# Second attention: blocks of a head from the last to the first, and the causal mask subtracted by VectorE

## The reference

```python
fcum = jnp.cumsum(log_f, axis=-1)
for blk in range(seqlen // ATT_BLOCK):                 # blocks of 128 queries
    q0, q1 = blk * ATT_BLOCK, (blk + 1) * ATT_BLOCK
    s = einsum(q[:, :, q0:q1], k[:, :, :q1]) * scale
    s = s + fcum[:, :, q0:q1, None] - fcum[:, :, None, :q1]
    s = jnp.where(kpos[None, :] <= qpos[:, None], s, -jnp.inf)
    prob = jax.nn.softmax(s, axis=-1)
    outs.append(einsum(prob, v[:, :, :q1]))
```

## Time and profile before

| | |
|---|---|
| time, median of 3 runs | 2604.86 us (2602.79 to 2605.42) |
| the profiled execution's own time | 2604.71 us |
| its span | 2602.9 us |
| granted clock of TensorE, mean | 0.991 |
| TensorE busy (matmul) | 2530.3 us, 97% of the span |
| TensorE weight loads busy | 2120.4 us, 81% |
| VectorE busy | 1580.3 us, 61% |
| ScalarE busy | 1225.1 us, 47% |
| GpSimd busy | 1134.3 us, 44% |

### The profile page before, as it was taken

The page is one execution under the profiler, slowest core; times in us unless marked ns, Lnnn a source line. Parts: engine busy times, 40 slices in busy tenths (PEclk is TensorE's granted clock), DMA queues, the critical chain, the costliest instruction groups (busy, mean ns, idle before and its releaser), DMA issues.

```text
span 2602.9 us, 32821 instructions
## 1 busy us (share of the span) xinstructions
PE 2530.3 (97%) x12946; PEld 2120.4 (81%) x12946; DVE 1580.3 (61%) x2413; ACT 1225.1 (47%) x1858; POOL 1134.3 (44%) x759
## 2 busy tenths in 40 slices
PE   5999999999999999999999999999999999999998
PEld 3788898877888888878788888888888888888886
DVE  7554899487555556665833367665666666654333
ACT  4243888344444443342543435543666666642132
POOL 0222444439787863444487234333322222235233
PEclk8999999999999999999999999999999999999998
DMA  6133001322222226553232322222111111167452
GB/s 272 65 121 130 1 1 66 114 79 92 89 81 78 92 102 242 179 174 122 90 117 102 122 73 90 90 84 71 65 49 49 49 59 60 54 213 273 148 184 97
DMA packets 84457, 275.81 MB, mean 106 GB/s; under 512 B 9392, under 2 KB 9520, under 8 KB 84304
## 3 DMA queue, kind: packets, MB, share of 16 engines
q1 hardware_dynamic: 84304, 273.71, 30.0%
HBM read 219.54 MB, written 54.13 MB: 105 GB/s over the span
## 4 chain that ended last, share of the span: by engine, by line
PE 81%; DVE 9%; ACT 5%; DMA 2%; issue 1%; POOL 1%; SPq 0%; DVEq 0%; ACTq 0%; POOLq 0%
PE ps L614 12%; PE ps L616 12%; PE ps L615 12%; PE ps L991 7%; PE ps L992 7%; PE ps L993 7%; PE ps L857 5%; PE ps L834 4%; PE ps L810 2%; PE ps L811 2%; PE ps L1048 2%; DVE wf L3056 2%; PE ps L1049 2%; PE ps L1050 2%; DVE wf L3081 1%
## 5 line engine op out<-in xcount | busy, mean ns | idle before, releaser
L3383 POOL TENSOR_TENSOR hl<-raw,hl 128x1024 fp32r<-128x1024 f32 x161 | 403.9, 2511 | 933.9 <-ACT hl L1407 933.5
L614 PE MATMUL ps<-ht,hl 128*128 128x512 f32 x1552 | 633.4, 408 | 15.0 <-DVE ht L2456 9.9
L616 PE MATMUL ps<-ht,hl 128*128 128x512 f32 x1552 | 608.3, 392 | 0.0
L615 PE MATMUL ps<-ht,hl 128*128 128x512 f32 x1552 | 607.8, 392 | 0.0
L614 PEld LDWEIGHTS ps<-ht,hl 128*128 128x128 f32 x1552 | 293.5, 189 | 75.4 <-DVE ht L2456 9.9
L616 PEld LDWEIGHTS ps<-ht,hl 128*128 128x128 f32 x1552 | 292.8, 189 | 64.1
L615 PEld LDWEIGHTS ps<-ht,hl 128*128 128x128 f32 x1552 | 294.0, 189 | 53.8 <-issue 1.5
L3459 POOL TENSOR_SCALAR wf<-wf,st 128x1024 f32<-128x1024 f32 (+2 forms) x192 | 168.8, 879 | 318.7 <-DVE st L2589 318.7
L1407 ACT ACTIVATE hl<-raw 128x1024 fp32r<-128x1024 f32 x163 | 171.3, 1053 | 178.9 <-PE ps L1050 66.6
L2396 DVE TENSOR_TENSOR ps<-ps,wf 128x512 f32<-128x512 f32 x116 | 80.8, 697 | 152.3 <-PE ps L993 152.1
L834 PE MATMUL ps<-cst,wf 128*128 128x128 f32 x1088 | 151.4, 274 | 3.8 <-POOL wf L3459 3.8
(11 more groups left out here) (287 smaller groups left out, 5314.8 us busy)
## 6 DMA issues: line engine op xcount, KB each, us to landing
raw<-in_wst SPq DMA_DIRECT2D x243, 512.0 KB, 3.6
wf<-scratch_rows SPq DMA_DIRECT2D x32, 512.0 KB, 5.0
scratch_g<-wf SPq DMA_DIRECT2D x22, 512.0 KB, 2.6
wf<-scratch_g SPq DMA_DIRECT2D x44, 256.0 KB, 4.2
wf<-in_xT SPq DMA_DIRECT2D x16, 512.0 KB, 7.7
htf<-in_wst SPq DMA_DIRECT2D x16, 512.0 KB, 15.4
scratch_ys<-wr SPq DMA_DIRECT2D x16, 512.0 KB, 4.5
ht<-scratch_ys SPq DMA_DIRECT2D x32, 256.0 KB, 5.9
```

The lines of the kernel that those rows point to most:

```text
L614: self.op.matmul(out, wh, xh[:, c], start=(j == 0), stop=False)
L615: self.op.matmul(out, wh, xl[:, c], start=False, stop=False)
L616: t = self.op.matmul(out, wl, xh[:, c], start=False, stop=(j == kt - 1))
L3383: self.op.tensor_tensor(K.hl[:, u * 2048 + 1024:u * 2048 + 2048], K.raw[:, i % 3 * 1024:(i % 3 + 1) * 1024], hi.bitcast(F32), ALU.subtract ...
```

## The change

Three things change, in the second attention only.

1. The matmul with `maskr` on line 815 is gone. VectorE instead subtracts `maskr` from the 128 diagonal columns of the head's running sums, in place, in a new function `mask(h, qt)`, which waits for the sums and for `maskr`; `top` now waits for the label `masked` of its block. Subtracting -1e30 there makes the sums large, and `top` subtracts the sums from the scores.
2. The blocks of a head go from 7 to 0. A block's piece of the tile, once masked, would spoil later blocks that read it unmasked; from the last to the first, each block reads only the pieces up to its own. The pairs for `back` are now (7, 6), (5, 4), (3, 2), (1, 0). VectorE masks block 7 of the pass's first head in step -2, before its first `top`, and after each `top` it masks the next block.
3. `fills` gives other numbers of filler steps to the steps of a pass. Passes 0 to 6 had 0, 2, 3, 3 in steps -2 to 1, and 1, 1, 2, 1, 2, 1, 1, 1, 2, 1, 2, 1 in steps 2 to 13. They now have 1, 2, 3, 3 and 1, 0, 1, 1, 2, 3, 3, 2, 1, 0, 0, 1. The last pass had 0, 3, 3, 3 and 2, 1, 2, 1, 2, 2, 2, 1, 2, 1, 2 (steps 2 to 12), and now has 1, 3, 3, 2 and 1, 1, 1, 1, 3, 3, 3, 2, 1, 1, 1.

```diff
--- before.py
+++ after.py
@@ -529,12 +529,12 @@
 
 
     if s < 2:
-        return (0, 3 if p == 7 else 2, 3, 3)[s + 2]
+        return (1, 3 if p == 7 else 2, 3, 3 if p < 7 else 2)[s + 2]
     if p == 7 and s > LAST_FILL:
         return {13: 1, 14: 4, 16: 3}.get(s, 0) if own else 0
     if p == 7:
-        return (2, 1, 2, 1, 2, 2, 2, 1, 2, 1, 2)[s - 2]
-    return 2 if s in (4, 6, 10, 12) else int(s < 14)
+        return (1, 1, 1, 1, 3, 3, 3, 2, 1, 1, 1)[s - 2]
+    return (1, 0, 1, 1, 2, 3, 3, 2, 1, 0, 0, 1)[s - 2] if s < 14 else 0
 
 
 def steps(n):
@@ -803,17 +803,11 @@
         for half in range((nk + 511) // 512):
             c = slice(half * 512, min(nk, half * 512 + 512))
             out = K.ps[pair][:, c]
-            diag = causal and c.stop == nk
             self.bank_free(2 * pair + half)
             for label in ready:
                 self.wait_ge(*K.at(*label))
             self.op.matmul(out, qs, K.wrr(kh)[:, c], start=True, stop=False)
-            t = self.op.matmul(out, qs, K.wrr(kl)[:, c], start=False, stop=not diag)
-            if diag:
-                self.consts()
-                self.wait_ge(*K.at("maskr"))
-                t = self.op.matmul(K.ps[pair][:, nk - 128:nk], K.idr[:, :], K.maskr[:, :],
-                                   start=False, stop=True)
+            t = self.op.matmul(out, qs, K.wrr(kl)[:, c], start=False, stop=True)
         t.then_inc(*self.done("scores", A, g))
         free = (("top", A, g),) if causal else (("exp", A, g),)
         for half in range((nk + 511) // 512):
@@ -839,9 +833,9 @@
     def back(self, A, g, qt, hi, lo, v, causal, ready, js=None, ahead=None):
 
         K = self.K
-        nk = qt + 1 if causal else 8
+        nk = (qt | 1) + 1 if causal else 8
         for gg in (g - 1, g):
-            for half in range((((qt if gg == g else qt - 1) + 1 if causal else 8) + 3) // 4):
+            for half in range(((qt + g - gg + 1 if causal else 8) + 3) // 4):
                 self.wait_ge(*K.at("plo", A, gg, half))
         for label in ready:
             self.wait_ge(*K.at(*label))
@@ -850,7 +844,7 @@
         if js[0] == 0:
             self.bank_free(b)
         for j in js:
-            c0 = 128 if causal and j == qt else 0
+            c0 = 128 if causal and j == nk - 1 else 0
             for n, m in enumerate((hi, lo)):
                 if ahead and (j, n) == (js[-1], 1):
                     self.wait_ge(*K.at(*ahead))
@@ -1284,7 +1278,7 @@
             def sc(s):
                 h = s // 8
                 k = 2 + 2 * h
-                self.scores(2, 16 * p + s, 2 * p + h, s % 8, h, k, k + 1, True,
+                self.scores(2, 16 * p + s, 2 * p + h, 7 - s % 8, h, k, k + 1, True,
                             (("stacklo", "q2", p, h), ("stacklo", "k", p, h),
                              ("stackhi2", "k", p, h)))
 
@@ -1296,11 +1290,11 @@
                     for _ in range(5):
                         next(late, None)
                 if 0 <= s < 16:
-                    self.turn(2, 16 * p + s, s % 8, 9 + (16 * p + s) % 3, True)
+                    self.turn(2, 16 * p + s, 7 - s % 8, 9 + (16 * p + s) % 3, True)
                 if s >= 2 and s % 2 == 0:
                     g = 16 * p + s - 1
                     hi, lo, _ = pt2(K, (g // 2) % 2)
-                    self.back(2, g, (s - 1) % 8, hi, lo, 6 + (s - 1) // 8, True,
+                    self.back(2, g, 7 - (s - 1) % 8, hi, lo, 6 + (s - 1) // 8, True,
                               (("vstack2", p),))
                 if p == 7 and s == LAST_FILL:
                     self.flush()
@@ -2211,13 +2205,13 @@
                 if g in (0, 2):
                     self.wait_ge(*K.at("stored_ys", 6 + g // 2))
                 if 0 <= s < 16:
-                    self.turn(2, g, s % 8, pt2(K, (g // 2) % 2)[0], True)
+                    self.turn(2, g, 7 - s % 8, pt2(K, (g // 2) % 2)[0], True)
                 if s + 2 < 16:
-                    self.soft(2, g + 2, (s + 2) % 8, 9 + (g + 2) % 3, True)
+                    self.soft(2, g + 2, 7 - (s + 2) % 8, 9 + (g + 2) % 3, True)
                 if s >= 2 and s % 2 == 0:
                     if s == 2 and p:
                         self.wait_ge(*K.at("stored_ya", p - 1))
-                    self.back(2, g - 1, (s - 1) // 8, (s - 1) % 8, w(22))
+                    self.back(2, g - 1, (s - 1) // 8, 7 - (s - 1) % 8, w(22))
                 if s == 15 and p < 7:
                     self.wait_ge(*K.at("scores", 2, g))
                     self.wait_ge(*K.at("qraw", p + 1, 1))
@@ -2573,14 +2567,23 @@
         if causal:
             pw = K.w(p)[:, 0:nk]
             if g >= 3:
-                self.wait_ge(*K.at("turn", A, g - 3, ((g - 3) % 8) // 4))
-            self.wait_ge(*K.at("fcum", h))
+                self.wait_ge(*K.at("turn", A, g - 3, (7 - (g - 3) % 8) // 4))
+            self.wait_ge(*K.at("masked", h, qt))
             self.op.tensor_tensor_reduce(pw, ps, K.w(20 + h % 2)[:, 0:nk], 1.0, -3.0e38,
                                          ALU.subtract, ALU.max, m).then_inc(*self.done("top", A, g))
             self.wait_ge(*K.at("top", A, g))
             self.op.tensor_scalar(m, m, -1.0, None, ALU.mult).then_inc(*self.done("minus", A, g))
         else:
             self.op.tensor_reduce(m, ps, AX, ALU.max, negate=True).then_inc(*self.done("top", A, g))
+
+    def mask(self, h, qt):
+
+        K = self.K
+        c = K.w(20 + h % 2)[:, qt * 128:qt * 128 + 128]
+        self.wait_ge(*K.at("fcum", h))
+        self.wait_ge(*K.at("maskr"))
+        self.op.tensor_tensor(c, c, K.maskr[:, :].bitcast(F32),
+                              ALU.subtract).then_inc(*self.done("masked", h, qt))
 
     def soft(self, A, g):
         K = self.K
@@ -3259,16 +3262,20 @@
                 g = 16 * p + s
                 self.fill(fills(p, s))
                 if s + 2 < 16:
-                    self.top(2, g + 2, 2 * p + (s + 2) // 8, (s + 2) % 8, 9 + (g + 2) % 3, True)
+                    if s == -2:
+                        self.mask(2 * p, 7)
+                    self.top(2, g + 2, 2 * p + (s + 2) // 8, 7 - (s + 2) % 8, 9 + (g + 2) % 3, True)
+                    if s + 3 < 16:
+                        self.mask(2 * p + (s + 3) // 8, 7 - (s + 3) % 8)
                 if late is not None and s + 2 >= 16:
                     for _ in range(5):
                         next(late, None)
                 if 0 <= s < 16:
-                    self.turn(2, g, s % 8, pt2(K, (g // 2) % 2), True)
+                    self.turn(2, g, 7 - s % 8, pt2(K, (g // 2) % 2), True)
                 if s + 2 < 16:
                     self.soft(2, g + 2)
                 if s >= 2 and s % 2 == 0:
-                    self.back(2, g - 1, (s - 1) // 8, (s - 1) % 8, w(22))
+                    self.back(2, g - 1, (s - 1) // 8, 7 - (s - 1) % 8, w(22))
                 if s == 15 and p < 7:
                     self.stack_low(w(23), (0, 1), (0, 1), ("q2", p + 1), 0.125)
                 if p == 7 and s == LAST_FILL:
@@ -3672,7 +3679,7 @@
                     for _ in range(5):
                         next(late, None)
                 if s + 2 < 16:
-                    self.weigh(2, g + 2, (s + 2) % 8, 9 + (g + 2) % 3, True)
+                    self.weigh(2, g + 2, 7 - (s + 2) % 8, 9 + (g + 2) % 3, True)
                 if p == 7 and s == LAST_FILL:
                     self.flush()
```

## The result

| | before | after |
|---|---|---|
| median of the runs, us | 2605.14 | 2628.02 (2626.35 to 2631.15) |
| ratio, 95% interval | | 1.0094 [1.0083, 1.0106] |
| profiled execution, own time, us | 2604.71 | 2626.35 |
| its span, us | 2602.9 | 2624.5 |
| from one store of `ya` to the next, us | 62.84 | 65.93 |

The change makes the kernel slower by 0.94%. The ratio and its interval are estimated from all runs of the two kernels, and so are not exactly the quotient of the two medians. The forecast was slower by 7.4 us, to 2612.1, in a range from 2600 to 2620. The spans of the profiled executions differ by 21.6 us, and 2628.02 lies outside the range.

A forecast was written before the change was run, and what follows sets the result against it. TensorE's instruction stream was taken as the bound: -14.1 us for masks, -2.4 for old waits gone, +22.5 for new waits in passes 0 to 6, +1.4 in the last pass, giving +7.4, 2612.1 us; range 2600 to 2620.

The forecast's parts named there:

- What bounds it: Second attention: TensorE's instruction stream is the time, busy 59.79 of 60 us; a wait put in is lost whole.
- Part 1: Line 815: removing 128 mask matmuls gives back 0.11 us each, -14.1 us in all.
- The rival of 0.06: Line 815: each mask matmul was worth its start distance alone, 0.06 us, so -7.7 us instead of -14.1.
- Part 2: VectorE's 128 new mask subtractions hold it 0.20 us each, 26 us, costing TensorE only where a low part is late.
- The mask is hidden there by 1.4 us or more: Pass start: the first mask fits between VectorE's last product copy and its first `top`, with 1.4 us or more spare.
- Part 3: Reversed block order and new filler places: still 32 filler steps a pass, no cost if nobody waits.
- Part 4: Bank 4 between turns, 2.06 us apart: waits in steps 12, 4, 2 and 10, together 3.2 us in passes 0 to 6.
- Step 2: Passes 0 to 6: the turn in this step waits 0.57 us for its half of bank 4.
- T(1) late behind ScalarE's weight tile: Step 1: ScalarE's 1.06 us weight-tile copy delays the turn's high part, starting 0.95 after the turn instead of 0.64.
- Only the bare distance: Rival: bank 4 waits count without queueing on the engines, 16.8 us against 16.5 gained, 2605 us; chance 0.24.
- No waits: Rival: the turns don't wait, -16.5 us, 2588 us; decides at 2.06 us of waits a pass; chance 0.16.
- Slower by more: Rival: mask matmuls worth only 0.06 us each, -7.7, and a mask operation of 0.28; 2619 us; chance 0.12.

The follow-up runs named there:

- old_order_no_mask: The kernel before without the mask matmul of line 815, mask left out altogether; 2595.85 us, ratio 0.9969.
- best1: The changed kernel with each pass's first mask moved ahead of VectorE's value stack and filler numbers chosen anew; 2599.67 us, ratio 0.9988.
- best1_pe_mask: best1 with the mask by TensorE's old matmul and no mask operation on VectorE; 2605.96 us, ratio 1.0010.
- no_dve_mask: The changed kernel with the mask left out altogether, neither matmul nor VectorE's subtraction; 2618.67 us, ratio 1.0061.
- order_alone: The kernel before with only the blocks' order reversed, mask matmul and old filler numbers kept; 2604.10 us, ratio 1.0003.
- halves_apart: The changed kernel with two filler steps moved so the 16th and 24th end a step (passes 0 to 6); 2618.12 us, ratio 1.0053.
- old_fills: The changed kernel with the filler numbers of the kernel before; 2607.32 us, ratio 1.0014.
- best1_split: best1 with the last store of `ya` issued between the fourth and fifth pair of loads; 2598.90 us, ratio 0.9979.
- best2: best1_split with a filler moved from step 13 to 10 in passes 0 to 6, and other last-pass numbers; 2593.69 us, ratio 0.9957.
- filler_in_12: The changed kernel with one filler step moved from step 8 to step 12 in passes 0 to 6; 2623.72 us, ratio 1.0080.

## Why the prediction was right on the side and wrong in the size

- **What bounds it.** Right. The waits put in were lost whole, as far as the table of starts can tell, which is to some 0.3 us of the 5.2 in a pass.
- **Part 1, -14.1.** Right as a price: 0.12 in old_order_no_mask where I had 0.11. The rival of 0.06 is out. The Trainium skill (TensorE: Matmul & The Clock Gate, Back-to-back issue gap) has 81 ns a matmul of 128 columns; the trace is nearer to 0.11. But a price isn't a gain: old_order_no_mask and best1 (against best1_pe_mask) each kept half of it a pass.
- **Part 2.** The hold of 0.20 was right (0.20 from mask to low part at 2008.71, and 0.2 at steps 4 and 12 in no_dve_mask). The duration was 0.282; the Trainium skill's formula (VectorE: DVE Perf Modes, the section on SBUF-source ops) gives 0.29, so it agrees. "The mask is hidden there by 1.4 us or more" failed: I had put the first mask between the stacks and `top`, which have the time, and did not look at GpSimd, which held it to 1.69. That cost 0.38 a pass at the scores and 0.20 at the copy in step 1. The trace of before already had operations on two SBUF operands that lasted more than three times as long beside GpSimd (L2868, in the section on hardware).
- **Part 3 is the step that failed.** "The fillers are still 32 steps a pass", it says, and "Reordering costs nothing if nobody waits." The order does cost nothing (order_alone). But I counted fillers as interchangeable steps of 0.7 us. They are halves of eight in one bank, and where a half ends inside a step TensorE waits for ScalarE: 1.90 a pass, some 13 us in seven, where the whole miss is 14.2. I had even worked out that 17 steps are done by the end of step 1, and read off it only that a weight tile is copied there. halves_apart shows it: the waits went when one filler step was moved across each of the two ends.
- **Part 4.** Right to 0.1 us in steps 12, 4 and 10. Step 2 was over-estimated by 0.38. The reason that I gave, T(1) late behind ScalarE's weight tile, is of a kind with what happened, but TensorE had stopped in step 1 already, and so ScalarE caught up before T(1). The part's list was of bank 4 alone.
- **Rivals.** "Only the bare distance" is out: steps 4 and 12 took 0.94 and 1.59, not 0.57 and 1.33. "No waits" is out: 5.2 us of waits a pass against the 2.06 from which it decides. "Slower by more" came out on its side and for another reason than it gave.
- **Last pass and after.** Forecast 1.4 of waits against 1.76 of masks, so shorter; measured 1.6 longer and 1.4 more behind it. In the last pass of after TensorE waits six times, 1.4 us for bank 4, 0.6 for L3227 (another hand-over of a half that the fillers make themselves) and 0.2 for the first `top`; with 0.15 for each place that is 3.1, less 1.76 for the masks. The store is issued 0.25 behind VectorE's last copy, since the loads are ahead of it. Together that gives the 1.6. The 1.4 behind it goes with the new wait of 1.8 for the reloaded `ya`: its store lands after 8.0 us, not 5.2. The prediction had no term for either.

The sum again, by the two profiled executions. Passes 1 to 6 were forecast at +1.1 and measured at +3.09 each: 11.9 more than forecast. The first pass grew by 2.2 (from its first scores, 1835.12 in after and 1837.26 in before, to its store): 1.1 more. The last pass and what follows it grew by 3.0 where 0.4 less was forecast: 3.4 more. That the second attention began 2.1 us earlier in after, in work that the change doesn't touch, takes 2.1 off. Together 14.3, and the miss is 14.2. Without that chance difference ahead of it the forecast would have been off by 2 us more.

## What to carry to other kernels

Before filler work is redistributed around a bound engine, write down for each buffer that this work itself hands over where in the sequence the hand-over falls, and keep other work of the engine between it and the next use; here two filler steps on the wrong side of it cost 10 us a kernel. Where an engine waits for a buffer's release, compute the distance through the engines that release it, with what queues on each: it gave three of the four waits here to a tenth of a microsecond, and work moved into one of them was free. And when instructions are taken off an engine that runs close to such distances, the distances have to be re-opened in the same change, or part of the gain turns into waits, here half of it in two pairs of kernels.

## What the runs showed of the hardware

**A VectorE operation on two SBUF operands that starts during a GpSimd operation lasts until that one ends.** In after the first mask of a pass took 1.18 us in the first pass and 1.68 to 1.70 in the seven others, instead of 0.28; the one shown above ended 0.15 behind GpSimd's L3390. Short GpSimd operations do it in small: a mask at 1986.15 took 0.38, beside a weighing of 0.59 that began at 1985.81. Of the 128 masks of after 71 began during a GpSimd operation, and every one of them ended 0.12 to 0.26 behind it; no mask that began outside one took more than 0.30. The same stands in the trace of before, in a subtraction of 512 columns with both operands in SBUF (the view of its line):
```profile
L2868 DVE TENSOR_TENSOR wr<-wf,wr x44: 678/2474/2886, 973.0 to 1198.8; 128x512 fp32r<-128x512 f32 x44
```
It takes 0.68 or 0.69 by itself, and 2.3 to 2.9 where it begins during GpSimd's L3383, ending some 0.55 behind it. Which of the two starts first decides. In best1, a usual pass, VectorE first:
```profile
2036.07 0.28 DVE L2585 TENSOR_TENSOR wf<-wf,maskr 128x128 f32<-128x128 f32 x1
...
2036.17 2.45 POOL L3389 TENSOR_TENSOR hl<-raw,hl 128x1024 fp32r<-128x1024 f32 x1
```
and the one pass that was 0.87 longer, GpSimd first:
```profile
2097.71 2.40 POOL L3389 TENSOR_TENSOR hl<-raw,hl 128x1024 fp32r<-128x1024 f32 x1
...
2097.98 2.27 DVE L2585 TENSOR_TENSOR wf<-wf,maskr 128x128 f32<-128x128 f32 x1
```
Against GpSimd's start VectorE's differs by 0.37 us, and the price by 2 us, with the next turn late. old_fills has a mask of 2.29 at 2100.34 in the same way and that pass is 1.4 longer; halves_apart, best1_split and best2 have one such pass each as well (2.44, 2.27 and 2.29 us; 1.3, 0.9 and 0.9 longer). The Trainium skill (GPSIMD Engine Reference, Specifications) says that GpSimd and VectorE share their SBUF interface and contend when VectorE reads two SBUF inputs; the trace agrees, and shows the size here. A low part, with one operand in PSUM, isn't held: the two at 1979.39 in after took 1.16 together, as in the earlier trace rows, all inside a GpSimd operation of 2.39 from 1978.30. So the move of the mask from TensorE, where the 128 matmuls of before lasted 0.22 to 0.28 us each, to VectorE brought a cost that depends on a race of tenths of a microsecond.

**A store right behind sixteen loads lands late.** SyncE's queue took 9.1 to 9.6 us to issue the loads, of 256 KB each. The store of 512 KB issued right behind them landed after 8.2 us in best1, 8.0 in after and 7.7 in order_alone, and its reload was issued 8.0 to 8.5 behind it. With 4.0 us between the last load and the store (before) it landed after 5.2, and with only eight loads ahead of it and eight behind (best1_split) after 4.0. The queue itself held the store for less: 0.85 us in best1, 0.25 in after, and in filler_in_12 it held it for none and the reload was still 8.0 behind. That the store's data wait behind those of the loads fits this, but no run here shows it by itself.
